# Two edits to a two-block transformer kernel: how the feed-forward layers behind a mixer begin, and how the first modulation vectors are made

## The reference, cut to what matters

```python
def first_block(x, c, ...):
    c_act = jax.nn.silu(c)
    for l in range(DEPTH):                                   # 2
        mod = (c_act @ w_ada[l] + b_ada[l]).reshape(b, N_MOD, 1, D_MODEL)     # 9 vectors of 1024
        sh1, sc1, g1, sh2, sc2, g2, sh3, sc3, g3 = [mod[:, i] for i in range(N_MOD)]
        h = modulated_norm(x, norm_g[l, 0], sh1, sc1)        # rmsnorm(x) * g * (1 + sc) + sh
        x = x + 0.5 * g1 * swiglu(h, ffn_wg[l, 0], ffn_wu[l, 0], ffn_wd[l, 0])
        h = modulated_norm(x, norm_g[l, 1], sh2, sc2)
        m = attn_pool_mixer(h, ...) if l % 2 == 0 else short_conv_mixer(h, ...)
        x = x + g2 * m
        h = modulated_norm(x, norm_g[l, 2], sh3, sc3)
        x = x + 0.5 * g3 * swiglu(h, ffn_wg[l, 1], ffn_wu[l, 1], ffn_wd[l, 1])
    return x

def swiglu(h, wg, wu, wd):                                   # 1024 -> 2816 -> 1024
    return (jax.nn.silu(h @ wg) * (h @ wu)) @ wd
```

## Time and profile before

| | |
|---|---|
| median of three executions | 2608.23 us |
| the profiled execution | 2614.62 us |
| its span | 2613.0 us |
| PE busy | 2478.3 us, 95% |
| DVE, ACT, POOL busy | 1630.6, 1080.0, 315.1 us |
| granted clock of PE, mean of the span | 0.973 |
| read from memory | 476.55 MB, 183 GB/s |

### The profile page before, as it was taken

How to read it: one execution, slowest core, us unless ns; L and a number is a source line. 1 busy time by engine, 2 the same in 40 slices (tenths; PEclk the granted TensorE clock), 3 DMA queues, 4 the chain that set the end, 5 groups by cost and what they waited for, 6 DMA issues and landing times.

```text
span 2613.0 us, 35873 instructions
## 1 busy us (share of the span) xinstructions
PE 2478.3 (95%) x13317; PEld 2118.1 (81%) x13317; DVE 1630.6 (62%) x1759; ACT 1080.0 (41%) x1223; POOL 315.1 (12%) x425
## 2 busy tenths in 40 slices
PE   7999988999999899999998999899999999998998
PEld 7777857887888788888798888788788898887886
DVE  3887347767875555555566675645545657757455
ACT  3434335435434444444353334344344344254443
POOL 3110111101102000000005500000100016200000
PEclk9999979999999999999999999999999999999999
DMA  7996318967974466556543233556456331534554
GB/s 288 320 329 224 132 33 279 306 218 278 325 257 146 152 227 208 176 182 201 156 122 97 99 114 139 168 189 213 148 193 218 94 108 62 164 114 145 178 191 145
DMA packets 337379, 479.26 MB, mean 183 GB/s; under 512 B 19867, under 2 KB 280314, under 8 KB 337258
## 3 DMA queue, kind: packets, MB, share of 16 engines
q1 hardware_dynamic: 314458, 398.43, 46.6%
q0 software_dynamic: 22800, 79.23, 8.2%
HBM read 476.55 MB, written 1.05 MB: 183 GB/s over the span
## 4 chain that ended last, share of the span: by engine, by line
issue 53%; PE 33%; POOLq 5%; DVE 3%; POOL 2%; DMA 2%; ACT 1%; DVEq 1%; ACTq 0%
PE ps L920 10%; PE ps L922 10%; PE ps L921 10%; POOLq L891 3%; POOLq L895 2%; DVE w_lo L2030 1%; PE ps L1182 1%; POOL n_rstd L716 1%; DMA probs<-in_w_ada_dram 1%; DMA spare<-in_w_ada_dram 1%; PE ps L986 1%; DVE mix_mem L2133 1%; PE ps L1241 1%; ACT w_hi L1613 0%; POOL rstd L710 0%
## 5 line engine op out<-in xcount | busy, mean ns | idle before, releaser
L2030 DVE TENSOR_TENSOR w_lo<-raw,w_hi 128x2048 fp32r<-128x2048 f32 (+1 forms) x368 | 825.6, 2245 | 476.0 <-ACT w_hi L1613 472.3
L1613 ACT ACTIVATE w_hi<-raw 128x2048 fp32r<-128x2048 f32 (+1 forms) x368 | 689.0, 1873 | 386.9 <-PE ps L922 353.5
L920 PE MATMUL ps<-w_hi,x_hi 128*128 128x512 f32 x1424 | 571.6, 401 | 13.3 <-DVE x_lo L2042 7.7
L922 PE MATMUL ps<-w_hi,x_lo 128*128 128x512 f32 x1424 | 559.9, 393 | 0.0
L921 PE MATMUL ps<-w_lo,x_hi 128*128 128x512 f32 x1424 | 559.8, 393 | 0.0
L920 PE MATMUL ps<-x_hi,w_hi 128*128 128x256 f32 (+1 forms) x1152 | 338.3, 294 | 14.7 <-DVE w_lo L2030 11.9
L921 PE MATMUL ps<-x_lo,w_hi 128*128 128x256 f32 (+1 forms) x1152 | 331.1, 287 | 0.0
L922 PE MATMUL ps<-x_hi,w_lo 128*128 128x256 f32 (+1 forms) x1152 | 331.0, 287 | 0.0
L920 PEld LDWEIGHTS ps<-w_hi,x_hi 128*128 128x128 f32 x1424 | 270.8, 190 | 70.5 <-issue 10.4
L922 PEld LDWEIGHTS ps<-w_hi,x_lo 128*128 128x128 f32 x1424 | 270.6, 190 | 58.6
L921 PEld LDWEIGHTS ps<-w_lo,x_hi 128*128 128x128 f32 x1424 | 271.3, 190 | 54.1 <-issue 0.5
(11 more groups left out here) (403 smaller groups left out, 3085.5 us busy)
## 6 DMA issues: line engine op xcount, KB each, us to landing
raw<-in_w_in_dram SPq DMA_DIRECT2D x96, 512.0 KB, 4.6
raw<-in_ffn_w_gate_dram SPq DMA_DIRECT2D x90, 512.0 KB, 4.0
raw<-in_ffn_w_up_dram SPq DMA_DIRECT2D x90, 512.0 KB, 4.9
raw<-in_ffn_wg_dram SPq DMA_DIRECT2D x88, 512.0 KB, 4.6
raw<-in_ffn_wu_dram SPq DMA_DIRECT2D x88, 512.0 KB, 6.1
raw<-in_ffn_wd_dram SPq DMA_DIRECT2D x80, 512.0 KB, 4.9
raw<-in_ffn_w_down_dram SPq DMA_DIRECT2D x80, 512.0 KB, 4.0
spare<-in_w_ada_dram POOLq DMA_DIRECT2D x46, 512.0 KB, 6.5
```

Of the source, the lines that this page charges most:

```text
L920: pe.matmul(dst, wh, vh, start=start, stop=False, skip_group_check=True)
L922: return pe.matmul(dst, wl, vh, start=False, stop=stop_, skip_group_check=True)
L1613: f(w_hi[s][:, 0:n], raw[s][:, 0:n], ACT.Copy).then_inc(hi_ready, 1)
L2030: v.tensor_tensor(w_lo[s][:, 0:n], raw[s][:, 0:n], w_hi[s][:, 0:n].bitcast(F32), ALU.subtract)\
```

## The change: what it does

**At feed-forward layers 1, 3, 5 and 7** (`third=True`) PE multiplies the first half of the tokens by three chunks around the transposes of the second half: chunks 0 and 1 ahead of them, chunk 2 behind them, and only then chunks 0 and 1 for t = 1. Chunk 2 writes the bank of chunks 0 and 1, so silu and `made` of the first pair for t = 0 now come ahead of `back` on ACT and DVE. The layers 0, 2, 4 and 6 keep the old order (`third=False`).

**At the beginning** all 16 units go through DVE, through six landing buffers; PE only sums over the partitions (two times 8 matmuls of one column) and runs six matmuls of 512 columns whose result nobody reads. POOL's constants come ahead of its first transfers, some constants of DVE (`ident_b`, `inv_count`, `quads`) come behind the first two `w_lo`, and the chunk loads of SP start at `ada_used` 10 and 16 instead of 4 and 8. DVE makes `w_lo` of chunk 0 behind the two vectors instead of ahead of them, and still ahead of the first `x_lo_a`.

```diff
@@ landing buffers and the sequence of SP
-        GROUPS = ((0, 1, 0), (2, 6, 8), (8, 4, 56), (12, 5, 88), (17, 1, 128))
+        GROUPS = ((0, 2, 0), (2, 6, 16), (8, 4, 64), (12, 5, 96), (17, 1, 136))
...
-                    sp.wait_ge(ada_used, 4)
+                    sp.wait_ge(ada_used, 10)
                 load_gu(wg, wu, 0, 0)
                 if late:
-                    sp.wait_ge(ada_used, 8)
+                    sp.wait_ge(ada_used, 16)
@@ POOL
-            for u in range(LANDINGS):
-                first_unit(u, False)
-                first_unit(u, True)
...
+            for u in range(2 * KT):
+                if u >= ADA_SLOTS:
+                    pool.wait_ge(ada_used, u - ADA_SLOTS + 1)
+                ada_unit(u // KT, u % KT, landing(0, u)[0])
+                if u == 10:
+                    norm_power(0)
@@ PE, ffn
                 s0 = take()
                 x_ready(c, 0, 0)
                 gate_up(s0, 0, 0)
-                turn_x(c, 1, src)
+                if not third:
+                    turn_x(c, 1, src)
                 s1 = take(1)
                 x_ready(c, 0, 1)
                 gate_up(s1, 1, 0).then_inc(gu_ready, 1)
+                if third:
+                    turn_x(c, 1, src)
+                    s2 = take(2)
+                    made(0, 0)
+                    gate_up(s2, 0, 0)
                 x_ready(c, 1, 0)
                 used(gate_up(s0, 0, 1))
                 x_ready(c, 1, 1)
                 used(gate_up(s1, 1, 1))
 
-                pair(1, True)
+                pair(1, True, begun=third)
@@ PE, the beginning
+            first_sums(0)
+            turn_x(0, 0, xn)
+
+            pe.wait_ge(ada_used, KT + 4)
+            for _ in range(6):
+                pe.matmul(ps[:, 3, :], ident[:], flat(vpad)[:, 0:512], start=True, stop=True)
+            first_sums(1)
+            ffn(0, 0, xn, xn, 1, third=False)
@@ ACT, ffn (DVE the same with made(0, 0))
                 ahead(b + 3)
+                if third:
+                    silu(0, 0, None)
                 back()
-                silu(0, 0, None)
+                if not third:
+                    silu(0, 0, None)
                 ahead(b + 4)
                 silu(0, 1, b + 1)
@@ DVE, the beginning
-            for u in range(KT):
...
+            for u in range(2 * KT):
+                ada_unit(0, u)
                 dve.drain()
-                if u in (2, 3):
-                    square_moment(0, u - 2)
+                if u in (3, 4):
+                    square_moment(0, u - 3)
...
+            ahead(1)
             x_lo_a(0, 0)
             ahead(2)
+
+            v.tensor_reduce(quads[:, 0:32], ident[:].rearrange("p (c n) -> p n c", n=32), AX, ALU.add)
+            v.tensor_copy(ident_b[:], ident[:])
```

More of the change, by code:

```diff
@@ L1015, in gates, with pair @@
                         gate_sum(grp, n)
-                def pair(i, first=False, with_gates=False):
+                def pair(i, first=False, with_gates=False, begun=False):
                     s = take()
-                    made(i - 1, 0)
-                    gate_up(s, 0, 0)
+                    if not begun:
+                        made(i - 1, 0)
+                        gate_up(s, 0, 0)
                     made(i - 1, 1)
@@ L1178, in _, with first_sums @@
             pe.transpose(ps[:, 0, 256:328], b_rows[:, 1, :], ident[0:72, 0:72]).then_inc(rows_turned, 1)
-            def first_sums(m, src, rhs, first=False):
+            def first_sums(m):
+                pe.wait_ge(ada_used, KT * m + KT)
                 for t in range(KT):
-                    last = pe.matmul(ps[:, 2, KT * m + t:KT * m + t + 1], src[:, t * P:t * P + P], rhs,
-                                     start=(first and t == 0), stop=True, skip_group_check=True)
-                return last
-            pe.wait_ge(c_ready, 1)
-            for u in range(KT):
-                if u == KT - 2:
-                    turn_x(0, 0, xn)
-                    for m in range(2):
-                        pe.wait_ge(ada_used, KT - 1 + m)
-                        first_sums(m, ada_acc[:, m, :], ones[:, 0:1])
-                slot = LANDINGS + u % LANDINGS
-                pe.wait_ge(ada_landed[slot], 16 * (u // LANDINGS + 1))
-                k = 4 + u // 2
-                first_sums(u % 2, ada_raw[slot], c_act[:, k:k + 1], u == 0).then_inc(cols_used, 1)
-            ffn(0, 0, xn, xn, 1)
+                    last = pe.matmul(ps[:, 2, KT * m + t:KT * m + t + 1], ada_acc[:, m, t * P:t * P + P], ones[:, 0:1],
+                                     start=(m == 0 and t == 0), stop=True, skip_group_check=True)
+                last.then_inc(cols_summed, 1)
+            first_sums(0)
[5 more added lines that the diff above has]
+            ffn(0, 0, xn, xn, 1, third=False)
             def mix_a0():
@@ L2189, in mod_finish, with ffn @@
                 dve.drain().then_inc(mod_ready, 1)
-            def ffn(f_no, b, back, border, grp=None, params=None):
+            def ffn(f_no, b, back, border, grp=None, params=None, third=True):
                 def made(i, t):
@@ L2222, in ffn @@
                 ahead(b + 3)
+                if third:
+                    made(0, 0)
                 back()
-                made(0, 0)
+                if not third:
+                    made(0, 0)
                 ahead(b + 4)
@@ L2364, in _ @@
             dve.drain().then_inc(mod_ready, 1)
+            ahead(1)
             x_lo_a(0, 0)
             ahead(2)
+            v.tensor_reduce(quads[:, 0:32], ident[:].rearrange("p (c n) -> p n c", n=32), AX, ALU.add)
+            v.tensor_copy(ident_b[:], ident[:])
+            v.tensor_copy(cmask_b[:], cmask)
+            v.tensor_copy(win[0][:, 0, :], count_i[:])
+            dve.drain()
+            v.tensor_copy(quads[:, 32:P].rearrange("p (c n) -> p c n", n=32), bc(quads[:, 0:32].unsqueeze(1), (P, 3, 32)))
+            v.reciprocal(win[1][:, 0, :], win[0][:, 0, :])
+            dve.drain()
+            for n, width in enumerate(WINDOWS):
+                v.tensor_scalar(inv_count[:, n, :], win[1][:, 0, :], 1.0 / width, None, ALU.max)
             dve.wait_ge(params2_in, 9 * 16)
@@ L2828, in ln_border @@
                     return border
-                ffn(l * 2 + 4, B0, lambda: x_lo_b(3 * l + 6, 1), ln_border(l, 0), params=columns)
+                ffn(l * 2 + 4, B0, lambda: x_lo_b(3 * l + 6, 1), ln_border(l, 0), params=columns, third=False)
                 ahead(B_MIX + 3)
```

76 lines of the change are left out of this document (20 added, 56 removed).

## The result

| | before | changed |
|---|---|---|
| median | 2608.42 us (2608.07 to 2612.12, 4 executions) | 2631.30 us (2624.48 to 2633.25, 4 executions) |
| the profiled execution, its span | 2614.62, 2613.0 us | 2630.28, 2628.6 us |
| PE busy | 2478.3 us | 2469.7 us |
| granted clock, mean | 0.973 | 0.969 |

The ratio is 1.008 (95% interval 1.0059 to 1.01): 22.9 us slower by the medians, 15.6 us between the two profiled spans. Three slow executions in the experiments (3501.64 and 8541.94 us among before's, 2795.01 among those of e4) are left out of the ratios. The forecast was 2610.4, with 2599 to 2617 for 8 in 10; the time lies outside.

A forecast was written before the change was run, and what follows sets the result against it. PE, busy 95% of the span, was taken as the bound, so time counts only where PE waits or runs at the lower clock. +10 for three chunks and -7.8 for the beginning gave +2.2, so 2610.4 us, 2599 to 2617 for 8 in 10.

The forecast's parts named there:

- Part one: Three chunks around the transposes at layers 1, 3, 5 and 7: +10 us, from +2.6 to +16.2.
- The order: Chunk 2 for t = 1 starts 1.3 us later in layers 1 and 3, nothing in 5 and 7: +2.6 us.
- The clock: Slow matmuls after waits at the four layers: +6.0 us, and +1.4 for the new wait after chunk 0's t = 1 pass.
- the old row: Profile of before, layer 3: 3.4 us at clock 0.50 held 8 matmuls instead of 15, a loss of 1.7 us.
- Rival one: Three chunks cost only their order, 2.6 us, the clock stays up, the beginning brings 9.5: 2601.3 us; 22%.
- Rival two: The clock falls in both waits of each three-chunk layer: 16.2 us, less 7.8, gives 2616.6 us; 16%.
- Rival three: Chunk 2's pass is free as made is ready when the transposes end: 2594 us with the new beginning; 6%.
- Part two: The new beginning: -7.8 us, from -11.5 to -4, with PE starting t = 1 at 51.8 instead of 60.46.
- I take 6, nearer to the row without a crowd: At the beginning, chunk 1's second transfer issues at 33.9, takes 6 us of a possible 4.9 to 9.1, lands at 39.9.
- the crowded row: Profile of before, beginning: the slower transfer duration, 9.1 us, used as upper end for chunk 1's second transfer.
- the remainder of layer 0 is bound by PE as before and keeps it: After the beginning: the rest of layer 0 keeps the gain, put at -7.8 us in the sum.
- Rival four: The beginning brings nothing, since layer 0 then waits for its transfers: 2618 us; 6%.

The follow-up runs named there:

- e4: The changed kernel's beginning without its six unread matmuls, old order at every layer; 2614.27 us, 0.9995 of before.
- e1: The kernel before with three chunks at layers 1, 3, 5 and 7, old beginning; 2625.83 us, 1.0045 of before.
- e6: e1 with unread 512-column matmuls in its three waits; 2613.08 us, 1.0002 of before.
- e17: e1 with unread 512-column matmuls only behind the transposes; 2615.64 us, 1.0008 of before.
- e2: The changed kernel with the old order at every layer, so the new beginning alone; 2614.62 us, 1.0002 of before.
- e3: e1 with layers 5 and 7 set back to the old order; 2627.79 us, 1.0051 of before.
- e7: e1 with ACT and DVE splitting chunk 2 ahead of the second half's norm in layers 1 and 3; 2619.70 us, 1.0034 of before.
- e8: e1 with DVE making the second half's hidden tile ahead of w_lo of chunk 3; 2623.50 us, 1.0045 of before.
- e10: The kernel before with unread matmuls (20, 20, 18, 18) ahead of its transposes in layers 1, 3, 5 and 7; 2608.24 us, 0.9981 of before.
- e11: e1 with the orders of e7 and e8, DVE waiting for POOL's power before chunk 2, and unread matmuls in the waits; 2608.46 us, 0.9985 of before.
- e5: The changed kernel itself, run again beside the others on one chip; 2626.48 us, 1.0056 of before.
- e12: The changed kernel with the unread matmuls of e6; 2611.68 us, 0.9997 of before.
- e16: e2 with SP loading chunk 1 at 12 units used instead of 16; 2611.55 us, 0.9994 of before.
- e14: e2 with e16's load, DVE's constants ahead of w_lo of chunk 1, and layer 0's back and x_lo ahead of chunk 2; 2605.82 us, 0.9964 of before.
- e15: e14 with e10's unread matmuls in the old order's long wait; 2599.14 us, 0.9945 of before.
- e13: The layers of e11 with the beginning of e14; 2600.23 us, 0.9948 of before.

## Why the prediction was wrong, point by point

**Part one, forecast +10, measured +11.8 (e1).** The mechanism was as told, wait by wait: the transposes' wait at 2.2 us (2.4 forecast), `hid` 3.4 us behind them (3.8 forecast), then 2.1 (2.2 forecast); in layer 5 they are 2.15, 1.88 and 1.95 (2.6, 1.9 and 2.2). The sizes of the terms were a little low. The order was put at 1.3 in layer 1, e6's trace has 1.6. The clock was put at 1.7 from a wait of the old profile; the pass of chunk 2 lost 2.5, since all of its twelve matmuls fell into the slow stretch, where 8 had stood in the old row. In layers 5 and 7 the forecast was no order and 1.65 of clock, the traces have 2.5 and 1.9. Sum in the profiled execution: 4.2 + 4.2 + 2.5 + 1.9 = 12.8, as for the whole layers in the table. So this part is right in cause and sign, 2 to 3 us short in size. Rival one (order alone, 2.6) is refuted by e1 itself, and e6 and e17 show the clock beside it. Rival two (the clock falls in both waits, 16.2) is too large, and above e1's interval (8.4 to 15.2): only the wait behind the transposes costs. Rival three (the pass of chunk 2 comes free) is refuted by the 3.44 us ahead of it.

**Part two, forecast -7.8, measured +0.5 with an interval from -1.8 to +3.1 (e2). This is the step that failed.** Of the 8.7 us forecast at PE's start of t = 1, 3.8 came, and none of them shows at the end. The vectors were ready at 35.06 us (34.8 forecast) and the first pass began at 39.1 (38). The step that went wrong is "I take 6, nearer to the row without a crowd": the second transfer of chunk 1 took 13.44, and this is all of the 4.9 us by which t = 1 began later than forecast (56.66 instead of 51.8). The stretches of the changed kernel show the crowd (DMA share and GB/s are the last two):

```profile
22.50:31.46 8.96, 8.96 (x24) 5.43 (x25) 7.71 (x6) 0.00 (x0) 5.57 (x11) 1.00 0.97 356
31.46:44.93 13.47, 8.96 (x40) 6.92 (x38) 4.69 (x7) 4.70 (x10) 2.50 (x5) 0.75 0.99 344
```

From 31.05 to 33.42 SP issued four transfers of 512 KB (chunks 1 and 2) and POOL five (two of `b_ada` and three units); nine of them are 4.7 MB, and at 344 GB/s that is 13.7 us. They share the rate instead of landing in the order of their issue: three units that POOL issued behind it, at 32.38, 32.90 and 33.42, took 10.7, 12.0 and 13.0 us and landed at 43.1, 44.9 and 46.4, on both sides of it. The prediction had POOL's units beside it and left out that SP asks for chunk 2 at once, since its buffer is free. Even the crowded row, 9.1, was too low a bound.

The second failure is the sentence "the remainder of layer 0 is bound by PE as before and keeps it", and behind it the sum's assumption that what is gained there reaches the end. The transposes that end layer 0 begin at 247.77 in before's trace. In eight other traces of kernels with the old beginning (e1, e3, e6, e7, e8, e10, e11, e17), which have the same code up to there, they begin between 242.67 and 247.03, the nine having a mean of 244.7. In the five with the new one and chunk 1 loaded late (the changed kernel, e2, e4, e5, e12) they begin between 241.34 and 242.66, mean 241.9. So the profile of before had the slowest layer 0 of all, and the gain at this place is 2.8 us, not the 6.4 between the two profiles. At PE's start of t = 1 it was 3.5 us by the means of the same traces, so 0.7 is lost in the rest of layer 0. One execution can lose more: e16 was 6.0 us ahead of the old mean at t = 1, and 1.2 at the end of the layer. Between 60 and 240 us DVE waits for POOL's units in every trace, 12 to 16 us in all, and what differs is how much of it reaches PE as waits for `hid`: 0.7 us in e10, 4.2 before, 3.1 in e16. Before, DVE's timeline:

```profile
131.84 1.28 DVE L2133 SCALAR_TENSOR_TENSOR mix_mem<-out_sb,mix_mem 128x1024 f32<-128x1024 f32 x1 [2.83 <-DMA out_sb<-in_w_ada_dram]
134.23 1.29 DVE L2133 SCALAR_TENSOR_TENSOR mix_mem<-spare,mix_mem 128x1024 f32<-128x1024 f32 x1 [1.11 <-DMA spare<-in_w_ada_dram]
```

and PE then stood 2.80 us for `hid`. The 2.8 us that are left at the end of layer 0 don't show in e2's total (+0.5, and at best -1.8). Where they go isn't settled: in one place, layer 2, the four traces e2, e4, e14 and e16 are 0.4 us longer than before's (196.0 us instead of 195.6), and the rest drowns in the mixers. With the mended beginning (e14, e15, e13) the same transposes begin at 237.68, 233.07 and 231.95, and the gain stays to the end.

**Rival four** (the beginning brings nothing, 2618) was the case, with 6%. Its reason, the transfers, was the right one, mostly at another place: the landing of chunk 1 cost 4.9 us, the rest of layer 0 another 0.7.

**The rest.** 11.8 and 0.5 make 12.3 us; e5 has 14.6 and the first comparison 22.9. Some 5 us of the latter lie with before, whose median was 2608.42 there and 2613.2 to 2614.5 in the four later comparisons. The 15.6 us between the two profiles are 12.8 in the four layers, -6.4 in layer 0, 0.4 in layer 2 and 9.1 in three of the four mixers, whose code didn't change: they are 2.9, 3.2 and 3.0 us longer in the changed kernel, the latter two (layers 4 to 5 and 6 to 7) with more time at the lower clock: 30.7 us against 23.9, and 27.3 against 20.5. e5's trace has these two again, within 0.2 us. In the other traces the stretch from 1296 to 1649 us is from 2.7 us shorter than before's (e10, with 17.1 us at the lower clock) to 6.9 longer (e11, with 37.5), whatever the kernel. Why the clock falls more often there in one kernel than in another isn't settled. The interval of the forecast was too narrow for two traces whose unchanged stretches differ by 3 to 6 us each.

## What to carry to other kernels

Work moved into a wait is worth only what the next wait doesn't take: list what the moved step itself needs, on the other engines' streams, and check whether the low clock lies in somebody's shadow before and under the work that sets the end after. Estimate a transfer's landing from the bytes of all that is asked for around it, by all queues, over the rate, not from the duration of a lone one: here 13.7 us by the first and 6 by the second, where 13.4 were measured. A single profile of an unchanged stretch can be off by several us (5.1 of 248 in layer 0); read the same stretch in several executions before a gain of that size is believed. And where totals scatter by 5 us, read the changed layers themselves in the traces.

## What the runs showed of the hardware

- POOL's power over one column took 2.54 us instead of 0.56 while DVE ran `w_lo`, an operation with two tensor inputs from SBUF, and ended 0.4 us behind it (e7, layer 1; 2.53 in its layer 3). In e11, where DVE waits for the power first, it took 0.56. The Trainium skill, "GPSIMD Engine Reference", section 1 (Specifications), says that POOL's SBUF interface contends with such DVE instructions; the trace agrees, and shows 2.0 us for a power that stands on the path of the norm.
- Matmuls of 512 columns followed one another after 0.43 us at a granted clock of 0.50 and after 0.23 at 1.00. The Trainium skill, "TensorE: Matmul & The Clock Gate", Part 1, gives 426.7 ns and 215.7 ns; the trace agrees at 1.2 GHz and has 0.227 us at 2.4 GHz (a weight load goes with each matmul here; whether that is the difference wasn't tested).
- Matmuls whose result nobody reads, put where the clock matters, gave back 9.7 us (e17), and put where it doesn't, nothing (e4, the start of layer 1 in e10).
- A transfer issued 5.8 us sooner, among others still under way, landed 2.3 us sooner (e16 against the changed kernel).
- Matmuls in layer 1 of before ran at 1.2 GHz for part of the layer and in e15 at 2.4 GHz throughout, and the layer took 201.0 us in both: a low clock under a wait that ends later costs nothing.
